# A fused decoder layer in float32: the activation's high and low parts as one moving operand of 512 columns

## The chip, the cores and the metric

The kernel runs on one core of one Trainium2 chip. The metric is the device time of one execution in microseconds (us), the median of the runs shown. TensorE is "PE" in the profile, its weight loads "PEld", VectorE "DVE", ScalarE "ACT", GpSimd "POOL" and SyncE "SP".

## What is computed

One decoder layer of width 2048 on one sequence of 256 tokens, in float32, cut to what matters here:

```python
h = rms_norm(x, norm_mix); proj = h @ w_in       # 2048 x 14368: gMLP u and v, q k v, z, beta a, two gates
y_a = chunked_spatial_gating(gelu(gm_uv), ...)   # 1024 wide
q, k, v = silu(causal_conv4(dn_qkv))             # 16 heads of 128
o = gated_delta_rule(q, k, v, g, beta)           # chunks of 64 tokens, a triangular solve in each
y_b = rms_norm(o) * silu(dn_z)
x = x + (gate_a * (y_a @ w_branch_a) + gate_b * (y_b @ w_branch_b)) @ w_out
f_gate, f_up = split(rms_norm(x, norm_ffn) @ w_gate_up)     # 2048 x 11264
x = x + (silu(f_gate) * f_up) @ w_down                      # 5632 x 2048
x = x + sigmoid(rms_norm(x, ple_norm) @ w_ple_gate) * (p @ w_ple_proj)
out = rms_norm(x, norm_final)
```

## The kernel before

**Precision by splitting.** Every float32 product of a weight W and an activation x is made of three products in the fp32r format: W = whi + wlo and x = xhi + xlo, and the kernel adds whi·xhi, whi·xlo and wlo·xhi.

**Weights.** They come from HBM in "halves" of 512 KB: [128 rows, 2 K tiles, 512 outputs] (`HALF_K` = 2, `COLS` = 512). A ring of four slots (`RING`) holds each half three times: `raw` (loaded by SP, `load_half`, L239), `whi` (a copy on ACT, `split_hi`, L245, L253) and `wlo` (a subtraction on DVE, `split_lo`, L255, L261). ACT and DVE split the half that lies three ahead (`LEAD`) of the one that PE uses. ACT may overwrite a slot only when PE has used the half four before (`half_used`), and SP may load it when DVE has split that one (`lo_done`).

**PE.** Activations lie transposed in SBUF, [128 features, K tile, 256 tokens], as two tensors each (`ahi`/`alo`, `yahi`/`yalo`, `ybhi`/`yblo`, `mhi`/`mlo`, `fhi`/`flo`, `phi`/`plo`). `use_half` (L263) waits for the half and issues, for each of its 2 K tiles and 4 tiles of 128 outputs, three matmuls with a 128x128 weight tile as the stationary operand and 256 tokens as the moving one:

```python
nc.tensor.matmul(o, wh, xhi[:, k], ...)   # L284
nc.tensor.matmul(o, wh, xlo[:, k], ...)   # L285
nc.tensor.matmul(o, wl, xhi[:, k], ...)   # L286
```

All three add into the same 256 columns of PSUM. Two accumulators `acc` of 1024 columns alternate, and one takes a block of 512 outputs. Only gMLP's v is computed the other way round (`rows=True`, L272 to L278): there the activation is stationary and 512 weight columns move.

**Stages in order.** qkv: four groups of four heads, each with blocks K, Q and V of 8 halves, in accumulators 0, 1, 0; between the halves PE, ACT, DVE and POOL carry the delta rule of the group before, in an order written out by hand (`FINISH`, `FIRST`, `START`, keyed by the number of the half). Part of it is an inversion: DVE makes `negm` (L1288), ACT stores and reloads it by DMA (L959 to L973), POOL inverts in 31 steps (L426 to L439), ACT stores and reloads the result (L975 to L987, landing in `diagT`), and PE merges it (`merge32_a`, L652) after half 5 of the next group. PE's `gram_q` (L622) after half 22 waits for `kbeg` (DVE, L1300). Then uv, z, mix (per 512 outputs: gate a, gate b, branch a of 4 halves, branch b), out, ffn (11 times a gate block and an up block), down, proj (4 blocks of one half) and ple.

**Evacuation.** When a block is full, DVE reads it from PSUM: `evac` (L1194) in qkv, `times_row` (L1488, L1492) where a norm's row factor R is multiplied in, L1538 where a residual is added, L1560 for ffn's up block, L1572 for proj. Then it frees the accumulator (`acc_read`), ACT applies the activation function, and ACT and DVE split the result into its high and low part for the next stage (`take_lo`, L1497). Each engine takes its instructions strictly in the order written, splits of weights among them. At the start (L1172 to L1192) DVE multiplies x by the norm's gain, ACT makes `ahi`, and DVE makes `alo`.

Of the kernel before, what the change touches and what calls it, by code (L numbers as in the profile page):

```python
# [24 lines left out]
ds = bass.ds  # L25
# [14 lines left out]
COLS = 512  # L40
HALF_K = 2
# [6 lines left out]
HFF = KF // HALF_K  # L48
NB = D // COLS
# [10 lines left out]
PLAN = [("qkv", 4, 3 * HID, (2, 1)), ("uv", 1, 4 * HID, (2, 2)), ("z", 2, 2 * HID, (1, 1)),  # L60
        ("mix", NB, 3 * HID + HGM, (2, 2)), ("out", 2, 2 * HID, (1, 1)), ("ffn", FB, 2 * HID, (1, 1)),
        ("down", 2, 2 * HFF, (1, 1)), ("proj", 1, 4, (2, 2)), ("ple", 2, 2 * HID, (1, 1))]
# [6 lines left out]
TOTAL = _h  # L69

# [12 lines left out]
def build(nc, win, wba, wa, wb, wo, wgu, wd, wpg, wpp, xT_d, pT_d, cols_d, hv_d, gmw_d, gmb_d, out_d):  # L83
# [21 lines left out]
    ahi = at("ahi", [P, KD, SEQ], F32R)  # L105
    alo = at("alo", [P, KD, SEQ], F32R)
# [44 lines left out]
    yahi = shared("yahi", [P, GMT, SEQ], F32R, 72)  # L151
    yalo = shared("yalo", [P, GMT, SEQ], F32R, 80)
    ybhi = shared("ybhi", [P, KD, SEQ], F32R, 40)
    yblo = shared("yblo", [P, KD, SEQ], F32R, 56)
    mhi = shared("mhi", [P, KD, SEQ], F32R, 0)
    mlo = shared("mlo", [P, KD, SEQ], F32R, 16)
    fhi = shared("fhi", [P, KF, SEQ], F32R, 0)
    flo = shared("flo", [P, KF, SEQ], F32R, 44)
# [17 lines left out]
    phi = at("phi", [P, PLE // P, SEQ], F32R, offset=pre_at)  # L176
    plo = at("plo", [P, PLE // P, SEQ], F32R, offset=pre_at + 2048)

    acc = [nc.alloc_psum_tensor(f"acc{n}", [P, 2, COLS], F32) for n in range(2)]
    ps = [nc.alloc_psum_tensor(f"ps{n}", [P, 2, COLS], F32) for n in range(2)]  # L180
# [5 lines left out]
    accv = [heads(a[:].rearrange("p a n -> p (a n)"), SEQ) for a in acc]  # L186
# [12 lines left out]
    x0_gain, x0_sq, x0_hi, x0_lo = sem("x0_gain"), sem("x0_sq"), sem("x0_hi"), sem("x0_lo")  # L199
# [3 lines left out]

    pre_done, conv_mac, conv_done, conv_silu = sem("pre_done"), sem("conv_mac"), sem("conv_done"), sem("conv_silu")
# [25 lines left out]
    res = [{k: sem(f"{k}{n}") for k in ("x", "sq", "gain", "added", "hi", "lo")} for n in range(2)]  # L230
# [32 lines left out]
    def use_half(pe, phase, i, n, buf, first, last, kt0, xhi, xlo, rows=False):  # L263


        s = n % RING

        pe.wait_ge(lo_done, half_of(phase, i, n) + 1)
        for kt in range(HALF_K):
            k = kt0 + kt  # L270
            begin, end = first and kt == 0, last and kt == HALF_K - 1
            if rows:  # L272
                for m in range(TILES):
                    xh, xl = xhi[:, k, m * P:(m + 1) * P], xlo[:, k, m * P:(m + 1) * P]
                    o = acc[buf][:, m]
                    nc.tensor.matmul(o, xh, whi[:, s, kt], start=begin, stop=False, skip_group_check=True)  # L276
                    nc.tensor.matmul(o, xh, wlo[:, s, kt], start=False, stop=False, skip_group_check=True)  # L277
                    mm = nc.tensor.matmul(o, xl, whi[:, s, kt], start=False, stop=end, skip_group_check=True)  # L278
# [37 lines left out]
    def tiles(ap, blk, j):  # L316

        return ap[:, ds(4 * blk + 2 * j, 2)]

    with nc.Block() as block:  # L320
# [3 lines left out]
        def _(sp):  # L324
            sp.dma_start(cols[:], cols_d).then_inc(cols_in, 16)
            for c in range(4):
                sp.dma_start(xT[:, 4 * c:4 * c + 4], xT_d[:, 4 * c:4 * c + 4]).then_inc(x_in[c], 16)
                load_half(sp, win, (BLK_K * HID + c) * P, c, c)
# [3 lines left out]
            def w_in_block(phase, i, blk, n0, skip=0):  # L332
                for n in range(skip, HID):
                    load_half(sp, win, (blk * HID + n) * P, half_of(phase, i, n0 + n), n0 + n)

            w_in_block("qkv", 0, BLK_K, 0, RING)
            w_in_block("qkv", 0, BLK_Q, HID)
            w_in_block("qkv", 0, BLK_DV, 2 * HID)
            with sp.Fori(1, NGROUPS) as g:
                w_in_block("qkv", g, BLK_K + g, 0)  # L340
                w_in_block("qkv", g, BLK_Q + g, HID)
                w_in_block("qkv", g, BLK_DV + g, 2 * HID)
            w_in_block("uv", 0, BLK_V, 0)
            w_in_block("uv", 0, BLK_V + 1, HID)
            w_in_block("uv", 0, BLK_U, 2 * HID)
            w_in_block("uv", 0, BLK_U + 1, 3 * HID)
            with sp.Fori(0, 2) as i:
                for b in range(2):
                    w_in_block("z", i, BLK_Z + 2 * i + b, b * HID)
            with sp.Fori(0, NB) as i:  # L350
                w_in_block("mix", i, BLK_GA + i, 0)
                w_in_block("mix", i, BLK_GB + i, HID)
                for n in range(HGM):
                    load_half(sp, wa, (i * HGM + n) * P, half_of("mix", i, 2 * HID + n), 2 * HID + n)
                for n in range(HID):
                    load_half(sp, wb, (i * HID + n) * P, half_of("mix", i, 2 * HID + HGM + n), 2 * HID + HGM + n)
            with sp.Fori(0, 2) as i:
                for n in range(2 * HID):
                    load_half(sp, wo, (i * (2 * HID) + n) * P, half_of("out", i, n), n)
            with sp.Fori(0, FB) as i:  # L360
                for b in range(2):
                    for n in range(HID):
                        load_half(sp, wgu, ((i + b * FB) * HID + n) * P, half_of("ffn", i, b * HID + n), b * HID + n)
            with sp.Fori(0, 2) as i:
                for n in range(2 * HFF):
                    load_half(sp, wd, (i * (2 * HFF) + n) * P, half_of("down", i, n), n)
            for n in range(NB):
                load_half(sp, wpp, n * P, half_of("proj", 0, n), n)
            with sp.Fori(0, 2) as i:
                for n in range(2 * HID):  # L370
                    load_half(sp, wpg, (i * (2 * HID) + n) * P, half_of("ple", i, n), n)
# [11 lines left out]
        def _(pool):  # L383
# [96 lines left out]
            with pool.Fori(0, FB) as i:  # L480
# [7 lines left out]
            for b in range(NB):  # L488
                for j in range(2 if b < NB - 1 else 0):
                    q = 2 * b + j  # L490
                    pool.wait_ge(ple_sig, q + 1)
                    if b == 0:
                        pool.wait_ge(pw_done, NB)
                    g.tensor_tensor(piece(t[0], j), piece(t[0], j), tiles(pw, b, j), ALU.mult).then_inc(ple_prod, 1)
                for j in range(2):
                    q = 2 * b + j
                    pool.wait_ge(ple_sq, q + 1)
                    if b < NB - 1:
                        g.tensor_tensor(sqsum[:], sqsum[:], piece(t[1], j), ALU.add).then_inc(sq_added, 1)
                    g.tensor_tensor(tiles(xT, b, j), tiles(xT, b, j),  # L500
                                    bc(cols[:, C_FIN + 4 * b + 2 * j:C_FIN + 4 * b + 2 * j + 2], SEQ), ALU.mult).then_inc(ple_gain, 1)
                    if b < NB - 1:
                        pool.wait_ge(sq_added, 9 + q)
# [7 lines left out]
        def _(pe):  # L511
            mm = nc.tensor.matmul

            def gemm(phase, i, n0, halves, buf, use, xhi, xlo, rows=False, after=None):
                acc_free(pe, phase, i, buf, use)
                for n in range(halves):
                    use_half(pe, phase, i, n0 + n, buf, n == 0, n == halves - 1, HALF_K * n, xhi, xlo, rows)
# [230 lines left out]
            def stages(d, g, n0):  # L748
# [3 lines left out]
                def put(n, f, *a):  # L752
                    if n0 <= n < n0 + HID:
# [13 lines left out]
            def group(g, d, extra=({}, {}), last=({}, {})):  # L767
                for p, buf, use in ((0, 0, 0), (1, 1, 0), (2, 0, 1)):
                    after = {n: (lambda fs: lambda: [f() for f in fs])(fs) for n, fs in stages(d, g, p * HID).items()}
                    if p < 2:  # L770
                        after.update(extra[p])
                        for n, f in last[p].items():
                            after[n] = (lambda a, b: lambda: (a(), b()))(after[n], f) if n in after else f
                    gemm("qkv", g, p * HID, HID, buf, use, ahi, alo, after=after)


            group(0, None, extra=({1: x_part(1), 3: x_part(2), 5: lambda: (x_part(3)(), first_sum()), 6: beta_a},
                                  {}), last=({}, {4: tok_columns}))
# [14 lines left out]
            for p, buf in ((0, 0), (1, 1)):  # L793
# [854 lines left out]
```

## Time and profile before

| | us |
|---|---|
| median of 3 runs | 1961.09 |
| lowest to highest | 1961.05 to 1963.62 |
| the profiled execution, its own time | 1959.92 |
| its span, first to last instruction | 1958.2 |
| PE busy in the span | 1895.7 (97%) |
| DVE, ACT, POOL busy | 1123.6, 838.8, 243.4 |
| mean granted clock of TensorE | 0.984 |

Busy time on PE counts overlapping matmuls once, and a matmul's end is modelled; how fast PE works is therefore read from the distance between the starts of neighbouring matmuls in the timeline. "L284" is line 284 of the kernel. In the answers "x" before a number is a count. The clock is given as a share of 2.4 GHz; the other level is 1.2 GHz.

### The profile page before, as it was taken

The page shows a single profiled execution, that of the slowest core. Times are in us where ns is not written, and L with a number is a line of the kernel's source. Part 1 is how long each engine was busy: PE and PEld are TensorE (multiplying, and loading weights), DVE is VectorE, ACT ScalarE, POOL GpSimd, SP SyncE. Part 2 cuts the span into 40 slices and gives each one's busy share as a digit, 9 for nine tenths or more (in the row PEclk, how much of TensorE's full clock was granted, in tenths as well). Part 3 has the DMA queues.
Part 4 walks back from the last instruction along what each step waited for, and adds up shares of the span by engine and source line. Part 5 has one row for each costly group of instructions (what it writes and reads, how often), then busy time and mean ns, then how long its engine had stood idle before and what let it go on. Part 6 is the DMA issues. An engine that isn't in the chain of part 4 may idle for free.

```text
span 1958.2 us, 39240 instructions
## 1 busy us (share of the span) xinstructions
PE 1895.7 (97%) x15550; PEld 1862.6 (95%) x15550; DVE 1123.6 (57%) x1265; ACT 838.8 (43%) x898; POOL 243.4 (12%) x369
## 2 busy tenths in 40 slices
PE   7989999998999999999999999999999999999996
PEld 6879898987999999999999999999999999999996
DVE  6675767674466545555566555555555545545565
ACT  4543443433545435444344444444444434434342
POOL 4060605143000000000011000000000000000033
PEclk9999999998999999999999999999999999999998
DMA  6343434444455555555555655555555555555442
GB/s 215 105 145 109 141 123 135 133 138 144 140 173 172 195 184 181 183 182 182 182 173 172 203 184 182 182 182 183 171 184 190 183 184 184 166 200 183 163 164 105
DMA packets 103129, 327.93 MB, mean 167 GB/s; under 512 B 23089, under 2 KB 23217, under 8 KB 103025
## 3 DMA queue, kind: packets, MB, share of 16 engines
q1 hardware_dynamic: 89024, 321.43, 49.4%
q10 hardware_dynamic: 13632, 3.67, 0.9%
q8 instruction: 81, 1.33, 0.3%
q0 software_dynamic: 368, 1.31, 0.2%
q14 instruction: 24, 0.19, 0.0%
HBM read 323.23 MB, written 3.15 MB: 167 GB/s over the span
## 4 chain that ended last, share of the span: by engine, by line
PE 82%; issue 8%; POOL 4%; DVE 3%; DMA 1%; ACT 1%; ACTq 1%; POOLq 0%; DVEq 0%; SPq 0%
PE acc L284 26%; PE acc L285 25%; PE acc L286 25%; POOL blk_x L437 2%; POOL blk_t L435 1%; DVE wlo L261 1%; POOL sqsum L417 1%; PE ps L565 1%; PE acc L276 1%; DMA diagT<-inv_out 1%; PE acc L277 0%; PE acc L278 0%; PE ps L571 0%; ACT whi L253 0%; DMA inv_out<-blk_xT 0%
## 5 line engine op out<-in xcount | busy, mean ns | idle before, releaser
L261 DVE TENSOR_TENSOR wlo<-raw,whi 128x1024 fp32r<-128x1024 f32 x604 | 755.8, 1264 | 719.7 <-ACT whi L253 714.6
L253 ACT ACTIVATE whi<-raw 128x1024 fp32r<-128x1024 f32 x604 | 629.9, 1055 | 849.4 <-PE acc L286 760.0
L284 PE MATMUL acc<-ahi,whi 128*128 128x256 f32 x3328 | 954.1, 287 | 22.2 <-DVE alo L1182 11.1
L285 PE MATMUL acc<-alo,whi 128*128 128x256 f32 x3328 | 947.0, 285 | 0.0
L286 PE MATMUL acc<-ahi,wlo 128*128 128x256 f32 x3328 | 946.7, 284 | 0.0
L284 PEld LDWEIGHTS acc<-ahi,whi 128*128 128x128 f32 x3328 | 644.0, 194 | 27.2 <-issue 21.6
L285 PEld LDWEIGHTS acc<-alo,whi 128*128 128x128 f32 x3328 | 644.3, 194 | 0.8 <-issue 0.7
L286 PEld LDWEIGHTS acc<-ahi,wlo 128*128 128x128 f32 x3328 | 644.2, 194 | 0.0
L284 PE MATMUL acc<-fhi,whi 128*128 128x256 f32 x704 | 199.2, 283 | 0.0
L285 PE MATMUL acc<-flo,whi 128*128 128x256 f32 x704 | 199.2, 283 | 0.0
L286 PE MATMUL acc<-fhi,wlo 128*128 128x256 f32 x704 | 199.2, 283 | 0.0
L284 PEld LDWEIGHTS acc<-fhi,whi 128*128 128x128 f32 x704 | 135.2, 192 | 0.0
L285 PEld LDWEIGHTS acc<-flo,whi 128*128 128x128 f32 x704 | 135.2, 192 | 0.0
L286 PEld LDWEIGHTS acc<-fhi,wlo 128*128 128x128 f32 x704 | 135.2, 192 | 0.0
L476 POOL TENSOR_TENSOR sqsum<-sqsum,t 128x512 f32<-128x512 f32 x16 | 26.4, 1650 | 849.6 <-ACT t L1111 849.0
L484 POOL TENSOR_TENSOR t<-t,R 128x512 f32<-128x512 f32 x22 | 28.2, 1304 | 455.7 <-ACT t L1125 455.7
L435 POOL TENSOR_TENSOR blk_t<-blk_m,blk_x 128x60 f32<-128x60 f32 (+24 forms) x124 | 53.3, 430 | 246.5 <-DMA blk_m<-inv_in 237.1
L284 PE MATMUL acc<-ybhi,whi 128*128 128x256 f32 x256 | 72.4, 283 | 0.0
L285 PE MATMUL acc<-yblo,whi 128*128 128x256 f32 x256 | 72.4, 283 | 0.0
L286 PE MATMUL acc<-ybhi,wlo 128*128 128x256 f32 x256 | 72.4, 283 | 0.0
L284 PE MATMUL acc<-mhi,whi 128*128 128x256 f32 x256 | 72.4, 283 | 0.0
L285 PE MATMUL acc<-mlo,whi 128*128 128x256 f32 x256 | 72.4, 283 | 0.0
(244 smaller groups left out, 1737.5 us busy)
## 6 DMA issues: line engine op xcount, KB each, us to landing
raw<-in_win SPq DMA_DIRECT2D x224, 512.0 KB, 3.4
raw<-in_wgu SPq DMA_DIRECT2D x176, 512.0 KB, 3.4
raw<-in_wd SPq DMA_DIRECT2D x88, 512.0 KB, 3.4
raw<-in_wb SPq DMA_DIRECT2D x32, 512.0 KB, 3.4
raw<-in_wo SPq DMA_DIRECT2D x32, 512.0 KB, 4.2
raw<-in_wpg SPq DMA_DIRECT2D x32, 512.0 KB, 3.9
raw<-in_wa SPq DMA_DIRECT2D x16, 512.0 KB, 4.2
xT<-in_xT SPq DMA_DIRECT2D x4, 512.0 KB, 7.3
```

The lines of the kernel that those rows point to most:

```text
L253: nc.scalar.activation(whi[:, s], raw[:, s], ACT.Copy).then_inc(hi_done, 1)
L261: nc.vector.tensor_tensor(wlo[:, s], raw[:, s], whi[:, s].bitcast(F32), ALU.subtract).then_inc(lo_done, 1)
L276: nc.tensor.matmul(o, xh, whi[:, s, kt], start=begin, stop=False, skip_group_check=True)
L284: nc.tensor.matmul(o, wh, xhi[:, k], start=begin and m % 2 == 0, stop=False, skip_group_check=True)
L285: nc.tensor.matmul(o, wh, xlo[:, k], start=False, stop=False, skip_group_check=True)
L286: mm = nc.tensor.matmul(o, wl, xhi[:, k], start=False, stop=end, skip_group_check=True)
L417: g.tensor_tensor(sqsum[:], sqsum[:], piece(t[1], q % 2), ALU.add).then_inc(sq_added, 1)
L435: chain(g.tensor_tensor(tmp, blk_m[:, j + 1:32, j:j + 1].to_broadcast([P, r, c]), blk_x[:, j:j + 1, 0:c].to_broadcast([P, r, c]), ALU.mult ...
L437: chain(g.tensor_tensor(blk_x[:, j + 1:32, 0:c], blk_x[:, j + 1:32, 0:c], tmp, ALU.add), v + 3 + 2 * j)
L476: g.tensor_tensor(sqsum[:], sqsum[:], piece(t[1], q % 2), ALU.add).then_inc(s["added"], 1)
L484: g.tensor_tensor(piece(t[1], j), piece(t[0], j), over(R[:], 2), ALU.mult).then_inc(ff_gate, 1)
L565: last = mm(psf[0][:, c:c + 1], tok_tile(src, h, m), ones[:, 0:1], start=True, stop=True)
```

## The change

The high and low part of each activation become one tensor with a leading index of 2 (`ax` [128, 2, 16, 256], and `ya`, `yb`, `mx`, `fx`, `px`). A matmul with a tile of `whi` now streams both parts, 512 columns (two strips of 256), into 512 columns of PSUM: the first 256 collect whi·xhi, the second whi·xlo. The matmul with `wlo` streams the high part alone into the first 256. An output tile thus takes 512 PSUM columns, so that a block has 256 outputs, and a half has 4 K tiles by 256 outputs (same bytes, same number of halves). ACT copies the second strip to SBUF (`low_part`), DVE adds the first to it (`sum_parts`), frees the accumulator and, where there is a row factor, multiplies by R in an instruction of its own. Residual blocks take two additions on DVE instead. `rows=True` keeps its three matmuls. In qkv there are six blocks a group, in accumulators 0, 1, 0, 1, 0, 1. proj is done in 8 pieces, of which four use the PSUM tensors `ps`. At the start ACT makes `ahi` from x with the gain as its scale, by K tile, and DVE makes `alo` in one instruction a K tile.

```diff
-COLS = 512
-HALF_K = 2
+COLS = 256
+WIDE = 512
+HALF_K = 4
+WIDE_K = 2
...
-    ahi = at("ahi", [P, KD, SEQ], F32R)
-    alo = at("alo", [P, KD, SEQ], F32R)
+    ax = at("ax", [P, 2, KD, SEQ], F32R)
+    ahi, alo = ax[:, 0], ax[:, 1]
...
+    def products(o, s, kt, m, x, k, begin, end):
+
+        wh, wl = whi[:, s, kt, m * P:(m + 1) * P], wlo[:, s, kt, m * P:(m + 1) * P]
+
+        nc.tensor.matmul(o, wh, x[:, :, k], start=begin, stop=False, skip_group_check=True)
+        return nc.tensor.matmul(o[:, 0], wl, x[:, 0, k], start=False, stop=end, skip_group_check=True)
...
-                for m in range(4):
-                    o = accv[buf][:, m]
-                    wh, wl = whi[:, s, kt, m * P:(m + 1) * P], wlo[:, s, kt, m * P:(m + 1) * P]
-
-                    nc.tensor.matmul(o, wh, xhi[:, k], start=begin and m % 2 == 0, stop=False, skip_group_check=True)
-                    nc.tensor.matmul(o, wh, xlo[:, k], start=False, stop=False, skip_group_check=True)
-                    mm = nc.tensor.matmul(o, wl, xhi[:, k], start=False, stop=end, skip_group_check=True)
+                begin, end = first and kt == 0, last and kt == HALF_K - 1
+                for m in range(2):
+                    mm = products(accv[buf][:, m], s, kt, m, x, HALF_K * h + kt, begin, end)
...
+            def low_part(phase, i, end, buf, dst):
+
+                acc_full(act, phase, i, end)
+                f(dst, accv[buf][:, :, 1], ACT.Copy).then_inc(low_taken, 1)
+
+            def pre_part(p, g):
+
+                if not (isinstance(g, int) and g == 0 and p < 2):
+                    act.wait_ge(conv_done, 12 * g + 4 * (p // 2 - 1) + 2 * (p % 2 + 1))
+                low_part("qkv", g, (p + 1) * HID, p % 2, piece(pre, p % 2)[:, :, 4:])
...
+                for n in range(GH):
+                    if n % HID == 0:
+                        pre_part((n // HID - 1) % 6, g if n else g - 1)
                     split_hi(act, "qkv", g, n)
...
+            def sum_parts(phase, n, buf, dst):
+
+                dve.wait_ge(low_taken, E0[phase] + n + 1)
+                v.tensor_tensor(dst, accv[buf][:, :, 0], dst, ALU.add).then_inc(part_summed, 1)
+                dve.wait_ge(part_summed, E0[phase] + n + 1)
+                dve.sem_inc(acc_read[buf], 1)
...
-                v.tensor_tensor(pre[:, :, 4:], accv[buf], over(R[:], 4), ALU.mult).then_inc(pre_done, 1)
-                dve.wait_ge(pre_done, 3 * g + p + 1)
-                dve.sem_inc(acc_read[buf], 1)
+                sum_parts("qkv", 6 * g + p, p % 2, piece(pre, p % 2)[:, :, 4:])
+
+            def scale_pre(p, g):
+
+                x = piece(pre, p % 2)[:, :, 4:]
+                v.tensor_tensor(x, x, over(R[:], 2), ALU.mult).then_inc(pre_done, 1)
...
+                    if n % HID == HID - 1:
+                        evac(n // HID, g)
+                        scale_pre(n // HID, g)
...
-                        for j in range(2):
-                            v.tensor_tensor(tiles(xT, 2 * i + b, j), piece(accv[b], j), tiles(xT, 2 * i + b, j), ALU.add).then_inc(s["x"], 1)
+                        x, part = tiles(xT, q), accv[b % 2]
+                        v.tensor_tensor(x, part[:, :, 0], x, ALU.add).then_inc(s["xh"], 1)
+                        dve.wait_ge(s["xh"], q + 1)
+                        v.tensor_tensor(x, part[:, :, 1], x, ALU.add).then_inc(s["x"], 1)
...
             def ffn(i, first=False):
+                for b in range(2):
+                    n, q, gate, up = 2 * b * HID, 2 * i + b, piece(t[0], b), piece(t[2], b)
+                    split("ffn", i, n, n + HID)
+                    sum_parts("ffn", 2 * q, 0, gate)
...
+                    v.tensor_tensor(gate, gate, over(R[:], 2), ALU.mult).then_inc(ff_scaled, 1)
...
+                    sum_parts("ffn", 2 * q + 1, 1, up)
+                    dve.wait_ge(ff_gate, q + 1)
+                    v.tensor_tensor(up, up, piece(t[1], b), ALU.mult).then_inc(ff_prod, 1)
+                    take_lo(fhi, flo, up, q, ff_hi, ff_lo)
...
+                f(ahi[:, k], xT[:, k], ACT.Copy, scale=cols[:, C_MIX + k:C_MIX + k + 1]).then_inc(x0_hi, 1)
```

## Rows read from the trace of the kernel before

**Rows 1.** The page: busy time of the engines; TensorE's granted clock in 40 slices.

```profile
PE 1895.7 (97%) x15550; PEld 1862.6 (95%) x15550; DVE 1123.6 (57%) x1265; ACT 838.8 (43%) x898; POOL 243.4 (12%) x369
...
PEclk9999999998999999999999999999999999999998
```

**Rows 2.** Busy time by stage; columns: stretch, length, five engines, PEclk, DMA share, GB/s.

```profile
225.00:331.00 106.00, 101.46 (x878) 97.55 (x876) 73.31 (x124) 43.88 (x48) 34.33 (x74) 0.98 0.43 134
655.00:975.00 320.00, 320.00 (x2669) 320.00 (x2668) 165.05 (x158) 141.62 (x144) 0.00 (x0) 1.00 0.55 182
1067.00:1575.00 508.00, 508.00 (x4232) 507.89 (x4231) 271.84 (x247) 213.86 (x225) 31.58 (x25) 1.00 0.55 182
1828.00:1850.00 22.00, 18.66 (x148) 18.46 (x147) 18.04 (x17) 8.51 (x10) 3.39 (x2) 0.92 0.43 140
1850.00:1958.00 108.00, 92.89 (x742) 90.17 (x740) 64.96 (x56) 41.87 (x48) 33.56 (x23) 0.93 0.41 138
```

**Rows 3.** PE's groups: line, operation, out<-in, shape, count; busy us, mean ns; idle before.

```profile
L284 PE MATMUL acc<-ahi,whi 128*128 128x256 f32 x3328 | 954.1, 287 | 22.2 <-DVE alo L1182 11.1 <-issue 5.8 <-DVE wlo L261 3.9
...
L284 PE MATMUL acc<-fhi,whi 128*128 128x256 f32 x704 | 199.2, 283 | 0.0
...
L284 PE MATMUL acc<-ybhi,whi 128*128 128x256 f32 x256 | 72.4, 283 | 0.0
...
L284 PE MATMUL acc<-mhi,whi 128*128 128x256 f32 x256 | 72.4, 283 | 0.0
...
L284 PE MATMUL acc<-yahi,whi 128*128 128x256 f32 x128 | 36.2, 283 | 0.0
...
L284 PE MATMUL acc<-phi,whi 128*128 128x256 f32 x32 | 9.7, 304 | 3.3 <-DVEq L1574 3.3
```

**Rows 4.** PE's timeline, 256-column matmuls in the out stage: start us, length, line.

```profile
999.72 0.28 PE L284 MATMUL acc<-mhi,whi 128*128 128x256 f32 x1
...
1002.96 0.28 PE L284 MATMUL acc<-mhi,whi 128*128 128x256 f32 x1
```

**Rows 5.** PE's timeline in the uv stage, `rows=True`.

```profile
439.20 0.39 PE L276 MATMUL acc<-whi,ahi 128*128 128x512 f32 x1
...
442.60 0.39 PE L276 MATMUL acc<-whi,ahi 128*128 128x512 f32 x1
```

**Rows 6.** PE's timeline in the proj stage.

```profile
1829.94 0.28 PE L284 MATMUL acc<-phi,whi 128*128 128x256 f32 x1
...
1833.34 0.28 PE L284 MATMUL acc<-phi,whi 128*128 128x256 f32 x1
```

**Rows 7.** Groups on DVE and ACT, columns as in rows 3.

```profile
L261 DVE TENSOR_TENSOR wlo<-raw,whi 128x1024 fp32r<-128x1024 f32 x604 | 755.8, 1264 | 719.7 <-ACT whi L253 714.6 <-DVE pre L1201 2.6 <-DVE t L1522 0.9
...
L253 ACT ACTIVATE whi<-raw 128x1024 fp32r<-128x1024 f32 x604 | 629.9, 1055 | 849.4 <-PE acc L286 760.0 <-issue 36.8 <-PE acc L278 28.3
...
L1492 DVE TENSOR_TENSOR t<-acc,R 128x512 f32<-128x512 f32 x54 | 34.8, 686 | 22.8 <-PE acc L286 22.8
...
L1542 DVE TENSOR_TENSOR t<-xT,cols 128x512 f32 x16 | 21.1, 1363 | 2.4 <-DVE xT L1538 2.4
...
L945 ACT ACTIVATE vnew<-ps 128x512 f32<-128x512 f32 x4 | 2.4, 594 | 0.1
```

**Rows 8.** PE's waits over the span: for whom; us in total, times, longest us.

```profile
PE ps L660 <- DMA diagT<-inv_out: 8.9, 3, 5.4
PE acc L284 <- issue: 5.8, 2, 3.1
PE ps L629 <- DVE kbeg L1300: 5.0, 4, 2.0
...
PE acc L284 <- DVEq L1574: 3.3, 1, 3.3
...
PE acc L284 <- DVEq L1203: 1.5, 1, 1.5
```

**Rows 9.** The chain that ended last: start us, us, what.

```profile
1939.25 0.70 DVE t L1492
```

More of the change, by code:

```diff
@@ L69 @@
 TOTAL = _h
+E0, _e = {}, 0
+for _name, _n in (("qkv", 6 * NGROUPS), ("uv", 4), ("z", NB), ("mix", 4 * NB), ("ffn", 2 * FB), ("ple", NB)):
+    E0[_name] = _e
+    _e += _n
 def half_of(phase, i, n):
@@ L266, in use_half @@
+    def use_half(pe, phase, i, n, buf, first, last, h, x, rows=False):
         s = n % RING
         pe.wait_ge(lo_done, half_of(phase, i, n) + 1)
-        for kt in range(HALF_K):
-            k = kt0 + kt
-            begin, end = first and kt == 0, last and kt == HALF_K - 1
+        for kt in range(WIDE_K if rows else HALF_K):
             if rows:
+                k = WIDE_K * h + kt
+                begin, end = first and kt == 0, last and kt == WIDE_K - 1
                 for m in range(TILES):
-                    xh, xl = xhi[:, k, m * P:(m + 1) * P], xlo[:, k, m * P:(m + 1) * P]
+                    xh, xl = x[:, 0, k, m * P:(m + 1) * P], x[:, 1, k, m * P:(m + 1) * P]
@@ L828, in _ @@
             pe.wait_ge(res[0]["lo"], 6)
-            gemm("ffn", 0, 0, HID, 0, 0, ahi, alo, after={4: next_sum(0), 5: operand_ready(res[0]["lo"], 8)})
-            gemm("ffn", 0, HID, HID, 1, 0, ahi, alo)
-            with pe.Fori(1, FB) as i:
-                for b in range(2):
-                    gemm("ffn", i, b * HID, HID, b, 0, ahi, alo)
-            pe.wait_ge(ff_lo, 2 * FB - 2)
-            gemm("down", 0, 0, HFF, 0, 0, fhi, flo, after={HFF - 3: operand_ready(ff_lo, 2 * FB)})
-            gemm("down", 0, HFF, HFF, 1, 0, fhi, flo)
+            first = {0: {2: operand_ready(res[0]["lo"], 8)}, 1: {0: next_sum(0)}}
@@ L837, in _ @@
+            for b in range(4):
+                gemm("ffn", 0, b * HID, HID, b % 2, b // 2, ax, after=first.get(b))
+            with pe.Fori(1, FB // 2) as i:
+                for b in range(4):
+                    gemm("ffn", i, b * HID, HID, b % 2, b // 2, ax)
+            pe.wait_ge(ff_lo, FB - 2)
+            for b in range(4):
+                gemm("down", 0, b * HFF, HFF, b % 2, b // 2, fx, after={HFF - 2: operand_ready(ff_lo, FB)} if b == 0 else None)
             with pe.Fori(1, 2) as i:
-                for b in range(2):
-                    gemm("down", i, b * HFF, HFF, b, 0, fhi, flo)
+                for b in range(4):
+                    gemm("down", i, b * HFF, HFF, b % 2, b // 2, fx)
@@ L850, in _ @@
+            pe.wait_ge(res[1]["lo"], 6)
+            first = {0: {2: operand_ready(res[1]["lo"], 8)}, 1: {0: next_sum(1)}}
+            for b in range(4):
+                gemm("ple", 0, b * HID, HID, b % 2, b // 2, ax, after=first.get(b))
+            for b in range(4):
+                gemm("ple", 1, b * HID, HID, b % 2, b // 2, ax)
+            pe.wait_ge(sq_added, 15)
             for k in range(2):
                 mm(psf[0][:, 0:SEQ], ones[:], sqsum[:, k], start=(k == 0), stop=False)
-            for j in range(2):
-                pe.wait_ge(ple_sq, 7 + j)
-                for k in range(2):
-                    last = mm(psf[0][:, 0:SEQ], ones[:], t[1][:, 2 * j + k], start=False, stop=(j == 1 and k == 1))
+            pe.wait_ge(ple_sq, NB)
@@ L856, in _ @@
+            for k in range(2):
+                last = mm(psf[0][:, 0:SEQ], ones[:], t[1][:, 2 + k], start=False, stop=(k == 1))
             last.then_inc(sq_summed, 1)
@@ L1411, in tok_copy @@
                 dve.sem_inc(ps_free, 1)
-            for n in range(3 * HID):
+            for n in range(GH):
                 split_lo(dve, "qkv", 0, n)
```

617 lines of the change are left out of this document (331 added, 286 removed).

## The prediction

> **What bounds the kernel now.** I read the page's busy shares first: PE is busy for 97% of the span, DVE for 57%, ACT for 43%, and TensorE's clock is granted in full nearly throughout [rows 1]. The busy time by stage sharpens this [rows 2]: in mix (655 to 975 us) and ffn (1067 to 1575 us) PE has no idle time, while DVE has half its time free and ACT more. In a qkv group (225 to 331 us), in proj and in ple PE idles for some us. So from the uv stage on, the time is the number of matmuls by the distance between them.
>
> That distance stands in the timeline. From one L284 to another 27 matmuls later 3.24 us go by [rows 4], 120.0 ns each. Streaming 256 columns at 2.4 GHz takes 106.7 ns; 13.3 ns are on top. With 512 columns, 15 matmuls take 3.40 us [rows 5], 226.7 ns each; streaming takes 213.3, and again 13.3 are on top. Between the two shapes, 256 more columns cost 106.7 ns and the surcharge does not grow: it is paid per matmul (each has a weight load of its own), not per column. This is the number on which the forecast rests.
>
> **The change, part by part.**
>
> *Fewer matmuls.* A group of three costs 3 x 120.0 = 360.0 ns. The pair costs one 512-column matmul and one of 256: 226.7 + 120.0 = 346.7 ns, so 13.3 ns less. The columns streamed are the same 768. The trace doesn't show the mixed pair, nor a moving operand of two strips 16 KB apart. Bounds: if the surcharge went with the columns, the pair would cost 360 (no gain); if each matmul paid only what the proj stage shows, where 30 matmuls take 3.40 us [rows 6], 113.3 ns each and 6.7 on top, the pair would be 213.3 + 106.7 + 2 x 6.7 = 333.3. I take 346.7, since rows 4 and 5 have the same operands as nearly all of the work and proj has 32 of the groups. The count is the sum of the six L284 groups [rows 3]: 4704. Of them qkv has 16 x 48 = 768 and proj 32; 3904 lie where PE has practically no idle time. 3904 x 13.3 ns = **52.1 us less**.
>
> The Trainium skill has a rule that speaks against this (TensorE: Matmul & The Clock Gate, "Back-to-back issue gap"): the isolated gap at full clock is the column count at 2.4 GHz plus 2.5 ns. By it a removed matmul would be worth 2.5 ns; the rows show 13.3, and what it would give is a rival below.
>
> *Added evacuation.* Each block of 256 outputs adds a copy on ACT from PSUM (0.59 us for 512 columns) and one or two instructions on DVE (0.69 each) [rows 7]. In ffn there are 44 such blocks: ACT 214 + 26 = 240 and DVE 272 + 30 = 302 of some 490 us. Both stay far from full, so the work itself costs nothing; what could cost is the delay at a block's end. There ACT copies (0.6), DVE adds and scales (1.4), ACT applies the function (0.6) and splits the next half (1.06), DVE splits it (1.26): 4.9 us, and with 0.1 for each of five handovers (my allowance) 5.4. PE holds three halves that are ready: 3 x 8 x 0.347 = 8.3 us. In residual blocks it is two additions, the gain (1.36 on average), two ACT instructions and the splits, 1.4 + 1.4 + 1.2 + 2.3 = 6.3 and handovers, 6.8. Neither empties the ring: cost nothing. If DVE were held up by another 1.5 us (the gain at its slow end), the residual blocks would begin to stall, 16 of them. The accumulator is free 2 us after its block, needed after 5.5 us at the earliest.
>
> *qkv.* Nominally 768 x 13.3 ns = 10.2 us would go. But PE isn't what limits all of a group: it waits for `diagT` at the merge (8.9 us in three times, [rows 8]), the end of negm, four DMAs, POOL's inversion and four DMAs more. None of that is shortened, so in the 15 of 24 halves from negm to the merge a faster PE only waits longer. The same goes for the removed boundary stall: V and the next K shared accumulator 0, and PE waited for `evac` (issue 5.8 and DVEq 1.5, [rows 8]); this goes, and what comes late next is `diagT`. What stays is 9 halves a group, about 1 us each. Against it: ACT's copies in front of the reload of negm (0.6 us a group); on DVE, which is busy for 73 of 106 us [rows 2] and already late at half 22, 1.4 us more before `kbeg` (5.0 us of waits, [rows 8], become some 12, most of it in the stretch that `diagT` bounds); and an evacuation of 2 us that DVE now does ahead of the k norm, at half 11. Longer waits may drop the clock. At the start, ACT and DVE lose a pass over x: 2 us less. Bounds 6 us less and 12 more; I take **3 us more**.
>
> *proj.* It takes 16.1 us from its first matmul to ple's, of which 3.3 are a wait for an accumulator behind DVE's residual work [rows 8], and the clock falls after it (mean 0.92, [rows 2]). Now four of eight pieces go to the free PSUM tensors. 32 pairs are 11.1 us; with about 0.4 + 1.0 us of waits left, **3.6 us less**. If DVE is later than I think, this is 0.
>
> *ple and the end.* The last block ends in one evacuation more (0.6 us) but one piece less; from the last block's first evacuation [rows 9] to the span's end, 19 us stay. Stalls for wlo (0.6 us in all) go. Nothing net.
>
> **Sum:** -52.1 + 3 - 3.6 = -52.7 on the profiled execution's 1959.9 gives 1907; its time is 1.2 below the median of the runs, so against that 1961.1 - 52.7 = **1908 us**.
>
> **The rivals.**
> 1. *The surcharge goes with the columns*, or two strips read slower. The pair costs 360. For it: proj's 113.3 ns and rows 5 are both 1/16 on top of streaming, 226.7 being twice 113.3. Against: ahi's own rows pay 120 at 256 columns. Only proj and qkv are left: 1961.1 + 3 - 3.6 = 1960. Chance 0.06.
> 2. *A matmul is worth 2.5 ns.* 3904 x 2.5 = 9.8 us: 1961.1 - 9.8 - 0.6 = 1951. This is the page's rule as a mechanism, surcharges tied to the weight stream and not to the number of matmuls. Chance 0.03.
> 3. *Slower: the ring runs dry at block ends.* ACT and DVE wait for each other in strict order, and the number of block ends doubles. It decides from a chain of 8.3 us; at 9.3 us PE loses 1.0 us at each of the 108 blocks of 256 outputs after uv. 108 - 52.7 gives 2016. Against: 5.4 to 6.8 us by the rows. Chance 0.04.
> 4. *Part of it:* DVE's full stretch in qkv costs 3 us a group more, and residual blocks stall. 1908 + 12 + some: 1915 to 1935. Chance 0.10.
> 5. *The surcharge is smaller in a pair*, as in proj: 3904 x 26.7 ns = 104 us less, 1857. Chance 0.06.
>
> **How the numbers follow.** The forecast has 0.71 (1890 to 1915). With rival 4 the range 1890 to 1935 holds 0.81; outside lie rivals 1, 2, 3 and 5. A difference of 0.2% (4 us) is about what a measurement of this kernel can tell from none. Faster: 0.71 + 0.10 + 0.06 + 0.03 = 0.90; same 0.06 (rival 1); slower 0.04 (rival 3).
>
> **What would show it.** In the timeline of ffn, distances from the whi to the wlo matmul and on of 227 and 120 ns, 347 for the pair; 240 and 120 would be rival 1. PE's records fall by 4704 matmuls (the count of the six groups). The busy time by stage should show ffn without idle time on PE, its length down by 3.7%, DVE near 60%. The ACT copy should take 0.6 us. In qkv, PE's wait for `diagT` should grow, those at group boundaries vanish, that for `kbeg` grow. In proj the wait should be near 1 us and the granted clock 1.00. If ffn's PE idles at block ends, the delay chain was mis-sized; if the whole gain is near 60, the qkv stage was less bound by the inversion than I read.

## The result: faster, by less than half of what was forecast

Device time, median of four runs each: before 1961.94 us (1961.05 to 1963.62), after **1937.93 us** (1930.08 to 1938.76). The ratio is 0.9869, 95% interval [0.9851, 0.9887]. The forecast was 1908 us, between 1890 and 1935. The kernel is faster, as said, but it gained 24 us where 53 were forecast, and its time lies 3 us above that range. The profiled execution took 1938.75 us (span 1937.0), 21.1 less than the profiled one of before (1959.9).

First the page of the changed kernel: engines, granted clock.

```profile
PE 1868.0 (96%) x10842; PEld 1611.6 (83%) x10842; DVE 1201.5 (62%) x1424; ACT 901.1 (47%) x1038; POOL 238.4 (12%) x371
...
PEclk9889899999999999999999999999999999999998
```

Against [rows 1] PE issues 4708 matmuls fewer (records) and is as busy. The work has gone, the time has not gone with it. The busy time by stage, columns as in [rows 2], with stretches of proj and ple at the end:

```profile
225.00:331.00 106.00, 102.33 (x666) 88.25 (x664) 73.05 (x130) 43.70 (x51) 27.30 (x64) 0.94 0.40 124
655.00:975.00 320.00, 320.00 (x1813) 277.44 (x1812) 191.47 (x195) 159.21 (x179) 0.00 (x0) 1.00 0.57 188
1067.00:1555.00 488.00, 488.00 (x2763) 423.25 (x2762) 290.08 (x284) 229.23 (x262) 28.53 (x22) 1.00 0.56 186
1815.00:1828.00 13.00, 11.76 (x65) 10.05 (x66) 10.58 (x14) 9.91 (x15) 1.33 (x1) 1.00 0.47 151
1828.00:1937.00 109.00, 92.85 (x517) 79.54 (x515) 74.38 (x66) 47.26 (x58) 40.22 (x25) 0.93 0.44 145
```

In mix and ffn PE has no idle time, as before: the doubled block ends cost nothing. The clock in proj is 1.00 (it was 0.92). In the qkv group it is 0.94 (it was 0.98). The groups of the matmuls and of the two new evacuation instructions, columns as in [rows 3]:

```profile
L283 PE MATMUL acc<-ax,whi 128*128 128x512 f32 x3328 | 1195.6, 403 | 13.6 <-DVE wlo L274 13.6
...
L284 PE MATMUL acc<-ax,wlo 128*128 128x256 f32 x3328 | 939.4, 282 | 0.0
...
L918 ACT ACTIVATE t<-acc 128x512 f32<-128x512 f32 x96 | 57.5, 599 | 153.8 <-PE acc L284 153.8
L1282 DVE TENSOR_TENSOR t<-acc,t 128x512 f32<-128x512 f32 x96 | 66.3, 691 | 93.3 <-ACT t L918 92.5
```

The copy takes 0.60 us and the sum 0.69, as [rows 7] had them. PE's timeline in ffn gives the distance between pairs:

```profile
1299.66 0.40 PE L283 MATMUL acc<-ax,whi 128*128 128x512 f32 x1
...
1306.73 0.40 PE L283 MATMUL acc<-ax,whi 128*128 128x512 f32 x1
```

These two are 20 pairs apart: 7.07 / 20 = **353.5 ns for a pair** (240 and 113 for its two matmuls), where the forecast had 346.7. Over longer stretches it is 353.3. Before, a triple took 360.0. So a group gained 6.7 ns, not 13.3.

The forecast's own value does occur, for a short while. From 559 to 575 us, in the last block of u and the first three halves of z, two matmuls 27 pairs apart are

```profile
565.81 0.39 PE L283 MATMUL acc<-ax,whi 128*128 128x512 f32 x1
...
575.17 0.40 PE L283 MATMUL acc<-ax,whi 128*128 128x512 f32 x1
```

9.36 / 27 = 346.7 ns, at a full clock. In qkv there are other such stretches. From 577 us on, after a wait of 1.5 us, every long stretch has 353.3, with the same operands in the rest of z. One placement thus has two values, and the kernel spends most of its time at the higher one.

The waits of PE in the changed kernel, columns as in [rows 8]:

```profile
PE ps L651 <- DVE kbeg L1391: 14.2, 4, 4.0
PE acc L283 <- DVE wlo L274: 13.6, 4, 11.0
PE ps L682 <- DMA diagT<-inv_out: 10.2, 4, 3.7
...
PE acc L283 <- DVEq L1661: 1.0, 1, 1.0
PE acc L283 <- DVEq L1627: 0.3, 1, 0.3
```

The wait for `kbeg` grew from 5.0 to 14.2 us. The stall at the group boundary is gone (L1203 in [rows 8]; of 5.8 us of issue none is left). Around proj 1.3 us remain of 3.3.

Where the two profiled executions part can be read from the start of single matmuls in their timelines. The "fourth merge" is the start of PE's `merge32_a` (L682) for the last group. It comes 11.5 us later than before (469.8 for 458.4). The fourth half of z, the first after the three that PE had ready, begins 8.1 us later (577.2 for 569.1). From there to proj the changed kernel is 23.3 us shorter, 3496 groups of 6.7 ns; proj is 3.1 shorter (13.0 for 16.1); ple and the end 2.9. Together 21.2 less. Two terms are off in these executions, then: the distance, and qkv. The experiments take them one after the other.

### The profile page after: what moved, and what is told of

The parts are those of the page before. It is cut to its first block, busy times and chain, and to the rows that moved or that the text cites. A ratio compares the mean times of both kernels' runs of the same rounds, so it can differ in the third digit from the quotient of the medians.

```text
span 1937.0 us, 30414 instructions
## 1 busy us (share of the span) xinstructions
PE 1868.0 (96%) x10842; PEld 1611.6 (83%) x10842; DVE 1201.5 (62%) x1424; ACT 901.1 (47%) x1038; POOL 238.4 (12%) x371
## 4 chain that ended last, share of the span: by engine, by line
PE 84%; DVE 7%; issue 3%; ACT 2%; DMA 2%; POOL 1%; ACTq 1%; DVEq 1%; SPq 0%; POOLq 0%
PE acc L283 51%; PE acc L284 26%; DVE wlo L274 2%; PE ps L587 1%; DMA diagT<-inv_out 1%; DMA inv_out<-blk_xT 1%; PE ps L593 1%; POOL sqsum L437 1%; DVE conv_v L1308 1%; ACT whi L266 1%; PE ps L651 1%; DVE conv_q L1308 1%; DVE pre L1282 1%; PE acc L299 1%; PE acc L301 0%
## 5 line engine op out<-in xcount | busy, mean ns | idle before, releaser
L283 PE MATMUL acc<-ax,whi 128*128 128x512 f32 x3328 | 1195.6, 403 | 13.6 <-DVE wlo L274 13.6
L284 PE MATMUL acc<-ax,wlo 128*128 128x256 f32 x3328 | 939.4, 282 | 0.0
L283 PEld LDWEIGHTS acc<-ax,whi 128*128 128x128 f32 x3328 | 631.8, 190 | 171.9 <-issue 13.0
L284 PEld LDWEIGHTS acc<-ax,wlo 128*128 128x128 f32 x3328 | 635.0, 191 | 0.8 <-issue 0.7
L283 PE MATMUL acc<-fx,whi 128*128 128x512 f32 x704 | 248.8, 399 | 0.0
L284 PE MATMUL acc<-fx,wlo 128*128 128x256 f32 x704 | 197.7, 281 | 0.0
L283 PEld LDWEIGHTS acc<-fx,whi 128*128 128x128 f32 x704 | 132.3, 188 | 33.1
L284 PEld LDWEIGHTS acc<-fx,wlo 128*128 128x128 f32 x704 | 133.0, 189 | 0.0
L283 PE MATMUL acc<-yb,whi 128*128 128x512 f32 x256 | 90.8, 399 | 0.0
L283 PE MATMUL acc<-mx,whi 128*128 128x512 f32 x256 | 90.5, 399 | 0.0
```

Source lines behind the costliest of these rows:

```text
L283: nc.tensor.matmul(o, wh, x[:, :, k], start=begin, stop=False, skip_group_check=True)
L284: return nc.tensor.matmul(o[:, 0], wl, x[:, 0, k], start=False, stop=end, skip_group_check=True)
```

## The experiments

Each figure is a single run unless a number of runs is named. On their chips the kernel before took 1960.84 us (e1 to e4), 1959.29 (m1, e5 to e7), 1961.04 (median of 11, e8 to e10) and 1960.80 (median of 11, e11 to e13). In the 400 us from 1100 to 1500 us, all ffn and free of idle time, distance is the stretch divided by the number of matmuls. The same stretch of six kernels, columns as in [rows 2]; before:

```profile
1100.00:1500.00 400.00, 400.00 (x3335) 400.00 (x3335) 209.71 (x191) 165.55 (x173) 20.50 (x16) 1.00 0.56 183
```

The changed kernel, then `e1_three`, `e2_contig`, `e4_before_pad` and `e5_before_pad64`:

```profile
1100.00:1500.00 400.00, 400.00 (x2266) 346.91 (x2265) 235.26 (x230) 185.02 (x213) 23.30 (x18) 1.00 0.57 187
```

```profile
1100.00:1500.00 400.00, 400.00 (x3336) 400.00 (x3335) 233.25 (x228) 183.30 (x211) 23.25 (x18) 1.00 0.55 181
```

```profile
1100.00:1500.00 400.00, 400.00 (x2266) 346.94 (x2265) 235.56 (x230) 184.99 (x212) 22.03 (x17) 1.00 0.57 187
```

```profile
1100.00:1500.00 400.00, 400.00 (x3532) 400.00 (x3531) 223.57 (x206) 175.85 (x185) 22.95 (x18) 1.00 0.59 192
```

```profile
1100.00:1500.00 400.00, 400.00 (x3398) 400.00 (x3398) 215.04 (x196) 168.77 (x178) 23.01 (x18) 1.00 0.57 186
```

Three matmuls by 400 / x: 359.8 before, 359.7 in e1, 339.8 in e4, 353.1 in e5. Two by 400 / 2266: 353.1 after and in e2.

**e1_three**: the 512-column matmul split in two again, all else as changed.

```
-nc.tensor.matmul(o, wh, x[:, :, k], ...)
+nc.tensor.matmul(o[:, 0], wh, x[:, 0, k], ...)
+nc.tensor.matmul(o[:, 1], wh, x[:, 1, k], ...)
```

> The change with its 512-column matmul split again into two of 256 (hi and lo strip), all else as in the change. Theory A (the surcharge is 16 cycles, 6.7 ns, for each 256-column strip read plus 16 per matmul): 360 ns per group of three, as in the kernel before. Theory B (what the pair costs has to do with 512-column matmuls or their write to PSUM, not with the count): another figure, 340 or 373 ns. Total by A: 1938 + 3904 x 6.7 ns = 1964 us; qkv as slow as in the change.

1966.44 us, 360.0 ns per group. The gain from z to proj goes with the one matmul: the stretch from the first matmul of out to that of proj takes 853.3 us, exactly as before. A group's gain is 6.7 ns, and blocks of 256 outputs bring nothing there by themselves. The loss in qkv is here too (fourth merge at 473.1 us, before 458.4), so it isn't the wide matmul's but the schedule's.

**e2_contig**: high and low part interleaved per K tile, so that the 512 columns lie in one piece.

```
-ax = at("ax", [P, 2, KD, SEQ], F32R)
+ax = at("ax", [P, KD, 2, SEQ], F32R)
```

> The change with high and low part of each K tile side by side in SBUF, so that the 512-column moving operand is one contiguous run and not two strips 16 KB or more apart. Theory A (each strip costs its own surcharge): the first matmul falls from 236.7 or 240 to 226.7 ns, the pair to 346.7 or less, total about 1912 us. Theory B (the surcharge goes with the columns streamed, 1/16, plus 16 cycles for each weight load): no change, 353.3 ns, total 1938. Theory C (it depends on where operands lie relative to each other): some other figure.

1930.36 us, inside the spread of the changed kernel, and 353.3 ns (346.7 in z up to 611 us). That the operand is two strips 16 KB apart costs nothing measurable.

**e3_pad**: the changed kernel with its activation operands 448 bytes further up in SBUF (`cursor[0] += 448` ahead of `ax`). **e4_before_pad**: the kernel before with the same line ahead of `ahi`.

> The change with all activation operands (ax and everything behind it) moved up by 448 bytes, which gives ax the position modulo 1024 bytes that the proj operand had in the kernel before (where 256 columns took 113.3 ns, not 120). Theory C (the surcharge is a matter of relative position of weights and moving operand): the 256-column matmul at 113.3 or less throughout, the pair at 340 or less, total about 1885 us; px, now at another position, slower. Theories A and B: 353.3 ns, 1938 us.

> The kernel before with the same shift of 448 bytes. Theory C: 113.3 ns instead of 120.0 for the 256-column matmuls, total 1962 - 4704 x 3 x 6.7 ns = 1867 us, and the proj matmuls at 120. Theories A and B: 120.0 ns and 1962 us, and proj's 113.3 ns stay unexplained.

e3: 1941.26 us and 353.3 ns, no gain; the stretches at 346.7 are gone. e4: **1906.21 us**, 353.3 ns in mix and most of z, and 340.0 in ffn and down. There one address takes 20 ns off a group of three, three times as much as the taking away of a matmul did. With three matmuls at 340 ns, the surcharge can't be a fixed price per matmul.

**e5_before_pad64**: the same with 64 bytes.

> The kernel before with the activations moved by 64 bytes (448 gave 353 ns in z and mix and 340 in ffn, 1906 us in all). If what matters is the position modulo 128 or 512 bytes against the weights, 64 does the same as 448: 1906 us; if the position modulo 1024, another total between 1870 and 1961; if it is a rhythm that any change of addresses upsets, nothing can be said but that it is not 360 throughout.

1934.47 us, 353.3 ns from z to down: a step of 6.7 from the 360.0 of no shift.

**m1_streams**, **m2_positions**, **m3_history**: nothing of the layer is computed; 24 groups to a section, from SBUF that no other engine touches during the stream, weights and moving operand at chosen distances.

> No layer is computed: one bare stream of matmuls on idle SBUF, in sections of 24 groups of weight tiles, each section with the pattern of the kernel before (T, three of 256), of the change (P, two strips; C, contiguous), single ones of 256 (S) or 512 (L) columns or weights moving (R), with the moving operand shifted by 0 to 448 bytes against the weights. Theory A (per strip and per matmul): T 360, P 353, C 347 ns, whatever the shift. Theory B (1/16 of the columns plus 16 cycles per weight load): T 360, P and C 353, S 120, L 220 to 227. Theory C (position): T differs between shifts, 340 to 360. Theory D (the surcharge comes from other engines' and DMA's traffic): 320 to 325 ns throughout.

Placement matters with all other engines idle, so it isn't their traffic. Three matmuls, from the first to the last group of a section: 360.0 ns with no shift (again 359.2 and 359.7 later), 353.5 at 64 bytes, 355.8 at 128, 341.1 at 192. Shifts 256 bytes further gave the same (359.2, 353.5, 355.8, 341.1). With the weights moved by 448 as well as the operand it was 359.0, and with the weights alone moved by 448, 353.5, what 64 bytes gave. So it is where the two lie to each other. Pairs gave 346.8 to 353.6.

Streams of one kind of matmul went opposite ways. Those of 256 columns took 119.6 ns each with no shift and 114.2 at 448; those of 512 columns 227.3 and 233.3. The shift that makes the short one cheaper makes the long one dearer.

> This kernel computes no part of the layer: it streams groups of matmuls from an idle SBUF, section by section, as the earlier one did, each section with the moving operand, its low strip or the low weights shifted by other numbers of bytes. Theory P (placement: the surcharge over 768 cycles comes from where weights and moving operand lie to each other, in steps of 16 cycles): the three-matmul group is again 360 ns at shift 0 and 341 at 192 and 448, and values between and below appear for the neighbouring shifts; for the pairs of matmuls there is a shift, or a shift of the strips to each other, with 340 ns. Rival Q (a 512-column matmul has a surcharge of its own that no placement takes away): no section of pairs comes under 346 ns, whatever is shifted, while three-matmul sections do.

No pair came under 346.4 ns in 26 sections of pairs, most with other shifts, other strip distances, or the low weights moved; three-matmul groups came to 340.8 again. But some placements had another value than in m1: 192 bytes now 353.4 for 341.1, two strips without a shift 353.5 for 347.0.

> This kernel computes no part of the layer: the streams of groups again, the same seven placements in changing order, at first without a pause between sections, then with about 2 us of idle TensorE ahead of each. Placement theory: each placement shows its one value wherever it stands (T0 360, T448 341, T64 353, T192 341 or 353, P0 347 or 353, C256 347 or 353). History theory: T0 and T448 keep their values, but T192, P0 and C256 show both of theirs, and which one follows from the section ahead (the value carries over) or changes from pause to pause.

One program now shows both values for one placement. PE's timeline in m3, first and last group of a section, 23 groups apart. Shift 192 behind a section at 340:

```profile
65.06 0.28 PE L99 MATMUL acc<-big 128*128 128x256 f32 x1
...
72.88 0.28 PE L99 MATMUL acc<-big 128*128 128x256 f32 x1
...
157.52 0.28 PE L183 MATMUL acc<-big 128*128 128x256 f32 x1
...
165.65 0.28 PE L183 MATMUL acc<-big 128*128 128x256 f32 x1
```

7.82 / 23 = 340.0 ns for the first section, and 8.13 / 23 = 353.5 for the second, which has the same operands but follows a section of pairs at 353.5. Shift 448, at 340.0 behind 192, was 353.4 behind a section of pairs at 353.6. Two sections with shift 64, each after 2 us of idle PE, settled at 353.3 and at 340.0. No shift gave 359 to 360 in every place (363.9 behind a pause, its slow first group included). That the surcharge depends on the placement, and that one placement can have two values, is shown. That what streamed before picks the value fits these sections, but nothing here shows by what rule; the mechanism stays open.

In m3 the granted clock also fell to half for three short times (0.50 from 345 to 348 us, for one). There a group took 640.0 ns, for shifts of 192 and 64 bytes and for pairs alike. That is its 768 columns at 1.2 GHz and nothing more: at half the clock no surcharge showed.

**e6_store_first**: the changed kernel; ScalarE issues the store of the inverse ahead of `silu_v`, and the reload one half earlier.

```
-FINISH = {2: (silu_v,), 3: (store_x,), 4: (load_diag,), ...
+FINISH = {2: (store_x, silu_v), 3: (load_diag,), ...
```

> The change with ACT's store of the inverse ahead of its SiLU of the V part (and the reload one half earlier). Theory Q1 (in qkv the change is slower because the store waits 5 to 8 us behind silu_v, which waits for DVE): diagT is there before PE, PE's wait at the merge (10.2 us in four) falls to under 5, and the first z matmul starts 3 to 8 us earlier than in the change (577.2 us). Theory Q2 (POOL's inversion bounds the group, as I predicted): no earlier start.

**e7_late_evac**: the changed kernel; evac(4) and its scaling move on VectorE from half 19 to half 21, behind `kbeg` and `decay_q`.

```
-                    if n % HID == HID - 1:
+                    if n % HID == HID - 1 and n != 19:
                         evac(n // HID, g)
                         scale_pre(n // HID, g)
+                    if n == 21:
+                        evac(4, g)
+                        scale_pre(4, g)
```

> The change with DVE's evacuation of block 4 (0.69 + 0.72 us) moved from before kbeg to after qdec, at half 21. Theory Q3 (the extra DVE instructions ahead of kbeg lengthen PE's wait): PE's wait for kbeg falls from 14.2 us in four to about 8.5, and the first z matmul starts 3 to 6 us earlier. Theory Q2 (bound by the inversion): the wait falls and the merge's wait grows by as much, same start.

1926.32 and 1919.38 us, the fourth merge at 460.8 and 451.6 us for the changed kernel's 469.8; distances 353.3 in both. In e6 the wait for `diagT` is gone, and the waits for `gb` (L971) are 10.2 us instead of 3.0. In e7 the wait for `kbeg` falls from 14.2 to 8.2 us. Single runs of a kernel that varies by 9 us in itself don't settle it. So the late sum was run again alone, and the store with it; the store alone was not.

**e9_late_store** (four runs): both edits together.

> The changed kernel with both reorders of the qkv stage: evac(4) and its scaling later on VectorE, store_x ahead of silu_v on ScalarE. If the two delays are one chain (late VectorE sum, so late conv_v, so late silu_v, so late store), the second reorder adds little once the first is there: 1915 to 1920 us. If they are separate delays their gains (18 and 12 us against the changed kernel) add: 1908 us. If moving the store only moves the wait to gb: 1920 to 1926.

1933.31 us, from 1931.56 to 1934.26: the third case of the expectation, and worse. The reason stands in its timeline, ACT and its queue in the second group:

```profile
242.14 2.59 ACTq L1035 DMA_DIRECT2D inv_out<-blk_xT  x4
244.85 1.06 ACT L983 ACTIVATE conv_v<-conv_v 128x1024 f32<-128x1024 f32 x1 [8.16 <-issue]
245.81 1.00 ACT L971 ACTIVATE gb<-ps 128x1024 f32<-128x1024 f32 x1
```

With the sum out of the way `conv_v` is ready early, but ACT now sits at the store until POOL's copy of the inverse (it starts at 241.32 us and takes 0.72), and `silu_v` and `gb` stand behind it; PE waits 17.1 us for `gb` instead. A wait was put ahead of work that didn't need it.

**e11_late_evac** and **e12_after** (five runs each, one chip): e7's kernel and the changed one.

> The changed kernel with evac(4) and its scaling later on VectorE, in five rounds. If the late sum costs the qkv stage its 11 to 18 us: 1920 us median, some 15 below the changed kernel on the same chip. If the single look of 1919 was the luck of one run: within 5 us of the changed kernel.

> The changed kernel once more, for a base on this chip: 1930 to 1939 us; group cadence again 353.3 ns, and a spread that comes from the qkv stage alone (merge 4 between 462 and 470).

Late sum 1924.44 us (1918.95 to 1927.62), changed kernel 1933.84 (1928.60 to 1938.36). The ranges do not touch, and **the late sum is worth about 9 us**, half of what the single run of e7 promised. The profiled runs' waits, e11:

```profile
PE ps L651 <- DVE kbeg L1391: 8.1, 4, 2.5
PE ps L682 <- DMA diagT<-inv_out: 7.9, 4, 3.2
```

and e12:

```profile
PE ps L651 <- DVE kbeg L1391: 13.7, 4, 3.8
PE ps L682 <- DMA diagT<-inv_out: 9.4, 4, 3.8
```

In e11 PE's waits for `kbeg` are 5.6 us shorter in sum than in e12, and those for `diagT` 1.5. The store of the inverse now follows POOL's copy sooner: in the four groups it trails the copy's end by 0.1, 0.1, 2.2 and 0.5 us in e11, by 0.1, 5.1, 2.2 and 4.5 in e12.

**e8_before_pad** (six runs) is e4's kernel; **e10_three_pad_late** (five) is the changed kernel with three matmuls, 448 bytes and the late sum; **e13_three_pad** (six) the same without the late sum.

> The kernel of before with its activation operands 448 bytes further up, timed in five rounds. Placement theory: 1906 us as in the single look, ratio 0.973 to the kernel before, so an edit of one address is worth more than the whole change. Rival (that look was a lucky run): 1930 us or more.

> The changed kernel with its 512-column matmul split in two again, operands 448 bytes further up and the later evac(4). Placement theory: 353 ns per group in z and mix and 340 in ffn and down, as the padded kernel of before, with the changed kernel's idle-free block ends, shorter proj and mended qkv stage: merge 4 at about 450, last matmul at 1875, 1890 us in all. Rival (the two-matmul form has its own worth beside the cadence): 1910 us or more.

> The changed kernel with three matmuls and the operands 448 bytes further up, without the later evac(4). If the late sum costs as much as in the changed kernel: 15 us above the version with both, 1908. If with shorter groups VectorE's sum matters no more or other waits bound qkv: within 4 us of 1893.

e8: **1893.16 us** (1885.84 to 1903.92), ratio to before 0.967 [0.9638, 0.9703]. e10: **1892.75 us** (1890.65 to 1897.38), 0.9664 [0.9645, 0.9683]. e13: 1896.24 us (1883.20 to 1906.31), 0.9655 [0.9616, 0.9694]. All three beat both kernels, and they can't be told from each other; so what the late sum is worth there is not shown. e8's runs fall into two bunches, three near 1886 and three from 1899 to 1904. Of this kernel there are two traces. The stretch 720 to 940 us (mix) in e4's run of 1906.21 us, and in e8's profiled one of 1886.50:

```profile
720.00:940.00 220.00, 220.00 (x1871) 220.00 (x1870) 115.88 (x112) 99.64 (x102) 0.00 (x0) 1.00 0.56 184
```

```profile
720.00:940.00 220.00, 220.00 (x1944) 220.00 (x1943) 121.14 (x117) 102.53 (x106) 0.00 (x0) 1.00 0.58 193
```

The same program, 3 x 220 / 1871 = 352.8 ns for a group in one run and 339.5 in the other: as in the streams, one placement has more than one value. z and mix have 1152 groups, and 13.3 ns for each are 15 of the 20 us between these two runs. Since the program is the same, the order of the stream alone doesn't fix the value. The profiled runs of e10 and e13 have 353.3 ns in mix. e8's comes nearest to 340.0 throughout, with 353.3 from z to down only between 1002 and 1051 us.

## Why the prediction was wrong in size and right in direction

**The cadence, the step that failed.** The text: the surcharge "is paid per matmul (each has a weight load of its own), not per column", so 3904 x 13.3 ns = 52.1 us. The reading rested on two shapes, 13.3 ns on both ([rows 4, 5]). In the changed kernel a pair takes 353.3 ns: 80 clocks of 2.4 GHz over its 768 columns (320.0 ns), where the triple had 96. 3904 x 6.7 ns is 26 us, and the timelines show 23.3 of them from z's fourth half to proj. Worse than the size was the model: three matmuls in 340.0 ns (e4, e8) have 20 ns of surcharge, half of "13.3 per matmul" and less than the pair's 33.3. What the runs show in its place is a surcharge that goes with the placement of weights and moving operand, and with the stream or the run besides. The pair at 346.7 exists (565 to 575 us), so the sum of the two matmuls wasn't impossible; taking it for the value of the whole kernel was the error. Rows of one placement can't separate a price per matmul from a price of the placement. The third row that I had, proj's 113.3 ns [rows 6], has another activation buffer; I kept it as an end of the bounds and took the value of the other two. It was the cue to ask what differs between the operands. The measured 353.3 lies within the bounds of the term (333.3 to 360), but no rival stood for the half of it, so the range ended at 1935, where half of 52.1 gives 1934 alone.

The rule of the Trainium skill (TensorE: Matmul & The Clock Gate, "Back-to-back issue gap") gives 2.5 ns over the columns for an isolated matmul, and by it removing one would save 2.5 ns. Measured, it saved 6.7 (e1 against the changed kernel). The measurement decides; the rule's figure is no guide to a stream at 360.

**The block ends: right.** Rival 3 (the ring runs dry) doesn't show: mix and ffn have no idle time on PE, with 0.60 and 0.69 us for the new instructions, and ACT and DVE ended near the forecast's share (290 of 488 us on DVE in ffn, 59%; "near 60%" was said). A group in ffn got shorter by 1.9% (360.0 to 353.3 ns), not 3.7%.

**qkv: direction right, reason wrong, size not settled.** I took +3 us, on the reading that `diagT`, behind POOL's inversion, bounds 15 of 24 halves. The wait for `kbeg` was said to become some 12 us (14.2) and the boundary stall to vanish (it did), but in the profiled run the fourth half of z began 8.1 us later. Before, the store waited for POOL's copy of the inverse and followed at once. The trace of before:

```profile
241.48 0.66 POOL L439 COPY blk_xT<-blk_x 128x256 f32<-128x256 f32 x1 [0.17 <-POOL blk_x L437]
...
242.39 2.69 ACTq L980 DMA_DIRECT2D inv_out<-blk_xT  x4
```

After, POOL was ready sooner and ACT wasn't there. The same place in the changed kernel's profiled run:

```profile
238.85 0.69 POOL L459 COPY blk_xT<-blk_x 128x256 f32<-128x256 f32 x1 [0.17 <-POOL blk_x L457]
...
247.04 1.06 ACT L983 ACTIVATE conv_v<-conv_v 128x1024 f32<-128x1024 f32 x1 [5.12 <-DVE conv_v L1308]
247.34 1.26 ACTq L1035 DMA_DIRECT2D inv_out<-blk_xT  x2
```

The store comes 7.8 us behind the end of POOL's copy, because ACT works in strict order and waits for `conv_v`, and DVE is late from the sums and scalings. That is the forecast's own remark "already late at half 22, 1.4 us more before `kbeg`", costed at nothing because "the stretch that `diagT` bounds" was to cover it; the cover was the thing being delayed. e11 shows the size: 1.4 us moved by two halves bring 9 us, over four groups, with shorter waits for `kbeg` and an earlier store. How these waits and the clock (0.94 in this group) share it isn't settled. The 8.1 us hold for this execution alone. By the medians the kernel gained 24.0 us here and 27.0 in e12. From z on the profiled executions show 29.3 gained, so by that some 5 and 2 us were lost ahead of it. The forecast's 3, less 152 groups at the measured 6.7 ns, would be 2.0, so the size of the term isn't refuted; e12's profiled run, its fastest, has the fourth merge at 460.8 us, 2.4 behind before.

**proj: right.** 3.1 us less for 3.6, wait 1.3 us, clock 1.00. **ple and the end:** 2.9 us less, of which 1.7 are its 256 groups at 6.7 ns; the forecast had 3.4 for the groups and nothing else.

In all, the forecast's -52.7 by place, against the profiled runs: up to z's fourth half +3 less 152 groups at 13.3 ns, +1.0, measured +8.1; from there to proj 3496 x 13.3 = -46.6, measured -23.3; proj -3.6, measured -3.1; ple -3.4, measured -2.9. Of the 31 us that are missing some 24 are the cadence and 7 the stages ahead of z.

## What to carry to other kernels

Before you price a change by the distance between instructions, measure that distance for more than one placement of the same operands: here one line that moves a buffer by 448 bytes was worth 68 us, the change itself 24. In an engine that works through its list in strict order, the cover of a delay must be checked for whether it starts behind that same list. And where a kernel's runs spread by 10 us, a single run of a variant is not a size: a reorder that promised 18 us was worth 9, and with one added that promised 12 the kernel was back at 1933 us.

## What the runs showed of the hardware

Unexpected: at a full clock TensorE's time for a group of 768 columns lay between 340.0 and 360.0 ns, at least 1/16 over the columns' 320.0 in every section and build. In the long stretches of the builds, three matmuls took 340.0, 353.3 or 360.0 ns and pairs 346.7 or 353.3. The value depends on the position of weights and moving operand relative to each other in SBUF (shift of 448 bytes: 360.0 to 341.1 ns; both shifted: 359.0), and shifts 256 bytes apart gave the same. It isn't fixed by that: the same operands gave 340.0 and 353.5 ns in one run (192 bytes), and the same program 340.0 and 353.3 in mix in two. Other engines' traffic isn't needed for it. At half the clock a group took 640.0 ns, the columns alone.

The Trainium skill (TensorE: Matmul & The Clock Gate, "Step-by-step: what each phase is for") says that weights and streaming operand have read ports of their own in SBUF, so that loading the next weights takes nothing from the running matmul. No run here looks at a port. But a stream whose time depends on where the two operands lie to each other (360.0 or 341.1 ns) shows that they aren't independent in time, at least for fp32r. A pair was never seen below 346.4 ns, while three of 256 columns reach 340.0; whether a pair can, stays open.
